# A mixture-of-experts pipeline: where silu and its product stand between the two halves of the next expert's gate and up weights

## The reference, cut to what matters

```python
xb = h[tok_b]
hid = jax.nn.silu(xb @ w_e_gate[e]) * (xb @ w_e_up[e])
return (hid @ w_e_down[e]) * w_b[:, None].astype(h.dtype)
```

## Time and profile before

| | |
|---|---|
| median of 3 runs | 3199.24 us (3198.63 to 3200.02) |
| the profiled execution | 3197.57 us, span 3195.9 us |
| PE busy | 2930.6 us, 92% of the span |
| DVE busy | 1774.6 us, 56% |
| ACT busy | 1414.9 us, 44% |
| POOL busy | 533.1 us, 17% |
| the experts' 64 blocks | about 1115 to 1752 us of the span |

### The profile page before, as it was taken

The page is one execution under the profiler, slowest core; times in us unless marked ns, Lnnn a source line. Parts: engine busy times, 40 slices in busy tenths (PEclk is TensorE's granted clock), DMA queues, the critical chain, the costliest instruction groups (busy, mean ns, idle before and its releaser), DMA issues. The chain is left out here.

```text
span 3195.9 us, 36485 instructions
## 1 busy us (share of the span) xinstructions
PE 2930.6 (92%) x14410; PEld 2346.5 (73%) x14410; DVE 1774.6 (56%) x2033; ACT 1414.9 (44%) x1832; POOL 533.1 (17%) x702
## 2 busy tenths in 40 slices
PE   7978899898998799999999679889999998889998
PEld 4856788787886387777777358678887797678887
DVE  4447745436544498888887253455544327455543
ACT  3324525336223188888787123433323225333322
POOL 0005514124101522222222100000000104000000
PEclk9989999998999799999999889999999999999999
DMA  5210101022652399999997632123332301223331
GB/s 199 60 55 1 56 32 54 27 54 73 211 191 92 114 338 365 364 370 370 373 373 304 261 113 93 53 81 92 105 105 66 96 27 54 73 80 93 93 105 40
DMA packets 276890, 455.94 MB, mean 143 GB/s; under 512 B 24400, under 2 KB 206288, under 8 KB 257648
## 3 DMA queue, kind: packets, MB, share of 16 engines
q1 hardware_dynamic: 250560, 398.82, 36.0%
q0 software_dynamic: 26160, 54.79, 4.8%
HBM read 450.63 MB, written 39.08 MB: 153 GB/s over the span
## 5 line engine op out<-in xcount | busy, mean ns | idle before, releaser
L253 DVE TENSOR_TENSOR weight_part<-weights,weight_part 128x2048 fp32r<-128x2048 f32 (+1 forms) x65 | 148.1, 2279 | 161.2 <-ACT weight_part L242 161.2
L1037 ACT ACTIVATE up_room<-banks,tap_columns 128x512 f32<-128x512 f32 x88 | 68.6, 779 | 314.0 <-PE banks L298 314.0
L293 PE MATMUL banks<-hT_r,weight_part 128*128 128x512 f32 x496 | 200.9, 405 | 4.6 <-PEq L878 2.9
L242 ACT ACTIVATE weight_part<-weights 128x2048 fp32r<-128x2048 f32 (+1 forms) x65 | 121.7, 1872 | 175.8 <-PE banks L293 169.9
L1078 DVE SCALAR_TENSOR_TENSOR up_room<-banks,tap_columns,up_room 128x511 f32<-128x511 f32 x88 | 65.9, 749 | 238.7 <-ACT up_room L1037 238.7
L298 PE MATMUL banks<-hT_r,weight_part 128*128 128x512 f32 x496 | 196.3, 396 | 0.0
L703 POOL TENSOR_SCALAR branch_mean<-branch_mean 128x1 f32<-128x1 f32 x20 | 4.4, 222 | 1113.2 <-ACT up_room L697 747.3
L293 PE MATMUL banks<-hT_r,weight_part_o 128*128 128x512 f32 x432 | 174.3, 403 | 7.1 <-PEq L110 4.2
L253 DVE TENSOR_TENSOR weight_part_o<-weights,weight_part_o 128x2048 fp32r<-128x2048 f32 (+2 forms) x49 | 106.9, 2181 | 129.5 <-ACT weight_part_o L242 129.5
L298 PE MATMUL banks<-hT_r,weight_part_o 128*128 128x512 f32 x432 | 170.5, 395 | 0.0
L297 PE MATMUL banks<-h_low,weight_part 128*128 128x512 f32 x432 | 169.7, 393 | 0.0
(11 more groups left out here) (704 smaller groups left out, 8746.3 us busy)
## 6 DMA issues: line engine op xcount, KB each, us to landing
weights<-in_w_e_gate SPq DMA_DIRECT2D x44, 1024.0 KB, 16.0
weights<-in_w_e_up SPq DMA_DIRECT2D x44, 1024.0 KB, 18.6
hT<-in_w_e_down SPq DMA_DIRECT2D x44, 1024.0 KB, 18.9
weights<-in_w_up SPq DMA_DIRECT2D x88, 512.0 KB, 5.1
gate_up<-in_w_e_gate SPq DMA_DIRECT2D x22, 1024.0 KB, 15.4
gate_up<-in_w_e_up SPq DMA_DIRECT2D x22, 1024.0 KB, 18.4
down<-in_w_e_down SPq DMA_DIRECT2D x22, 1024.0 KB, 18.8
weights<-in_w_down SPq DMA_DIRECT2D x20, 1024.0 KB, 5.0
```

Of the source, the lines that this page charges most:

```text
L242: c.nc.scalar.activation(self.parts[n % 2][0][:, 0:z], self.raw[n % RAW_SLOTS][:, 0:z], ACT.Copy).then_inc(self.high_ready, 1)
L253: c.nc.vector.tensor_tensor(low[:, 0:z], self.raw[n % RAW_SLOTS][:, 0:z], high[:, 0:z].bitcast(F32), ALU.subtract).then_inc(self.low_ready, 1)
L293: ins = c.nc.tensor.matmul(out, lhs[0], rhs[0], start=start, stop=False)
L1037: nc.scalar.activation(a[:, f % 2, v], c.ps[:, 2 * (f % 4) + v], ACT.Identity, scale=conv[:, 2, ch:ch + 1], bias=bias[:, ch:ch + 1]).then_ ...
```

## The change

In block n, ScalarE and VectorE now take the first half of block n + 1's gate and up weights ahead of silu and its product, and the second half behind them. What each instruction computes and the semaphores that it waits for and counts up are as before; TensorE, SyncE and GpSimd have the same lists.

```diff
-            def round_gate_up(n):
+            def round_half(n, v):
                 i = n % SETS
                 if n >= 2:
                     act.wait_ge(up_done, n - 1)
-                for v, landed in enumerate((gate_in, up_in)):
-                    act.wait_ge(landed[i], 16 * (n // SETS + 1))
-                    nc.scalar.activation(gu_high[n % 2][:, v], gu[i][:, v], ACT.Copy).then_inc(gu_rounded, 1)
+                act.wait_ge((gate_in, up_in)[v][i], 16 * (n // SETS + 1))
+                nc.scalar.activation(gu_high[n % 2][:, v], gu[i][:, v], ACT.Copy).then_inc(gu_rounded, 1)
...
                 if n + 1 < N:
-                    round_gate_up(n + 1)
+                    round_half(n + 1, 0)
                 if n < N:
                     act.wait_ge(up_done, n + 1)
                     if n >= 2:
                         act.wait_ge(gated, n - 1)
                     nc.scalar.activation(sl[n % 2][:], c.ps[:, n % 2, 0:EF], ACT.Silu).then_inc(silud, 1)
+                    if n + 1 < N:
+                        round_half(n + 1, 1)
                     round_down(n)
...
                 if n + 1 < N:
-                    part_gate_up(n + 1)
+                    part_half(n + 1, 0)
                 if n < N:
                     dve.wait_ge(silud, n + 1)
                     if n >= 2:
                         dve.wait_ge(hid_turned, n - 1)
                     nc.vector.tensor_tensor(hid[n % 2][:], sl[n % 2][:], c.ps[:, n % 2, EF:2 * EF], ALU.mult).then_inc(gated, 1)
+                    if n + 1 < N:
+                        part_half(n + 1, 1)
                     dve.wait_ge(d_rounded, n + 1)
```

More of the change, by code:

```diff
@@ L3331, in _ @@
                     nc.scalar.activation(by_row[:, tile, b * 64:(b + 1) * 64], c.ps[:, TURNED_AT[tile] + b].rearrange("p (q r) -> p q r", r=KD), ACT.Copy).then_inc(copied, 1)
-            round_gate_up(0)
+            for v in range(2):
+                round_half(0, v)
             for f in range(2):
@@ L3388, in _, with part_half @@
             hid_bank = c.ps[:, 2, 0:2 * P].rearrange("p (k n) -> p k n", n=P)
-            def part_gate_up(n):
+            def part_half(n, v):
                 i = n % SETS
-                for v in range(2):
-                    dve.wait_ge(gu_rounded, 2 * n + v + 1)
-                    nc.vector.tensor_tensor(gu_low[i][:, v], gu[i][:, v], gu_high[n % 2][:, v].bitcast(F32), ALU.subtract).then_inc(gu_parted, 1)
+                dve.wait_ge(gu_rounded, 2 * n + v + 1)
+                nc.vector.tensor_tensor(gu_low[i][:, v], gu[i][:, v], gu_high[n % 2][:, v].bitcast(F32), ALU.subtract).then_inc(gu_parted, 1)
             def part_x(n):
@@ L3502, in _ @@
             shared_gate(1)
-            part_gate_up(0)
+            for v in range(2):
+                part_half(0, v)
             for n in range(2):
```

## The result

The changed kernel takes **3236.24 us** (4 runs, 3233.06 to 3239.92) against 3199.63 us (3198.63 to 3202.61) of the kernel before: ratio 1.0115, 95% interval 1.0101 to 1.0129. The forecast was 3232, range 3222 to 3247. The profiled execution took 3238.21 us, span 3236.5 us.

The account below looks back on a forecast made before the run. TensorE was taken as the bound, with transfers at 0.96 in the middle stretch; the change adds a three-engine ring. +10.7, +16.1, +2.5 and +3.1 make +32.4 us, so 3199.24 becomes 3231.6, say 3232, range 3222 to 3247.

Parts of the forecast that it names:

- The ring: Each expert block: up product, then second half's rounding and low part behind silu, then next up product; 10.39 us per block.
- S + 4.59: Next up product's start, 4.59 us after S, when a block's up product is done; before, S + 3.61 in the early stretch.
- The three stretches: Added time: first 11 blocks (9.41 us each) +10.7, middle 49 (10.06) +16.1, last two (9.15) +2.5 us.
- The start: First block: next up product moves from 1122.89 to 1126.01, +3.1 us.
- The clock rival: Gaps in every block drop TensorE's clock, 1.6 us per fall: one block in four +25 us, all +99; chance 0.05.
- What stands behind the moved instructions: Later work on both engines still fits: ScalarE has 2.4 us to spare, VectorE's chain 0.2 us.
- Transfers at nothing: Weight transfers cost nothing, as slower blocks ask less of them; up weights land well under 19 us, DMA share about 0.92.
- The rival of late transfers on top: Late weights lengthen single blocks beyond 10.39 us: 16 blocks by 0.5 give +8, 3240 us; chance 0.12.
- the rival "hardly any change": Transfers alone set the middle stretch's 10.06 us and the ring is about 10.0: +11, 3210 us; chance 0.06.
- the wait at L3165: Middle stretch: hidden values' turning waits for the product of silu and up, 27 times, 23.3 us; removed but not gained.

Follow-up runs that it names:

- the first block as before: Changed kernel, but with the order of the kernel before in the first block (n = 0): 3232.34 us, ratio 1.0102.
- ScalarE's list alone: Kernel before with only ScalarE's list changed (second half behind silu), VectorE taking both halves and then the product: 3267.27 us, ratio 1.0218.
- the run without gathers: Changed kernel without the token gathers of blocks 4 to 63, computing on stale tokens: 3241.57 us, ratio 1.0135.
- VectorE's list alone: Kernel before with only VectorE's list changed (product between the halves), ScalarE rounding both halves before silu: 3199.76 us, ratio 1.0001.
- the runs with two pieces: Second half cut in two pieces: changed kernel with one TensorE wait 3200.12 us, with two waits 3196.32; order of the kernel before, two waits, 3199.37.
- the runs without gathers: Token gathers of blocks 4 to 63 left out: of the kernel before, 3172.85 us (ratio 0.9919), and of the changed kernel, 3241.57 us (1.0135).
- two pieces, one wait: Changed kernel with the second half in two pieces, TensorE waiting for all pieces at the up product's start: 3200.12 us, ratio 1.0003.

## Why the prediction was right, step by step

- **The ring.** Forecast S + 4.59 and 10.39 us per block; measured S + 4.62 and 10.45, and in the middle stretch no block lies outside 10.38 to 10.56. The links: 0.29, 1.91, 0.03, 2.29 and 0.10 for TensorE's start, which I had at 0.06 from the product's; the up product itself took 5.82 us instead of 5.80 (1203.63 to 1209.45).
- **The three stretches.** Forecast +10.7, +16.1 and +2.5 us. Blocks 1 to 11 took 1245.44 - 1127.95 = 117.49 us against 103.56, +13.9, of which 2.5 are the slow matmuls of block 1 (12.94 - 10.44); the middle stretch 512.18 - 492.99 = +19.2, the last two blocks 20.78 - 18.30 = +2.5. Without the slow matmuls the excess over the forecast, 0.7 and 3.1 us, is the 0.06 us per block.
- **The start.** Forecast +3.1 for the wait of the first block. It was mis-sized in one thing: the wait also dropped the clock, which the sum put at nothing. Up to block 1's up product the profiled execution lost 1127.95 - 1122.89 = 5.1 us. Of these 0.9 lay ahead of the blocks and 1.0 in block 0's up product, which ran at the lower clock for ten matmuls instead of four; both come before the moved half can act, and with the first block as before it was three matmuls. The other 3.2 are the wait, as forecast. Behind it come the 2.5 us of the slow matmuls. The clock rival priced a fall at 1.6 us with a chance of 5% and looked for it in the gaps of every block; it came in one place that I had not looked at. Everywhere else gaps of 0.8 us left the clock at 1.00: 61 of them in 637 us, and with ScalarE's list alone gaps of 1.3 us in every block did so too. The Trainium skill ("TensorE: Matmul & The Clock Gate", "A second HAM failure mode: psum-queue depth-cycling") reports for another kernel that short idles, when frequent enough, made the clock swing; it gives no length or rate for them, so this case doesn't contradict it, but no such swing occurred here.
- **How close the number is.** Forecast 3232, median 3236.24. The profiled execution is 2 us above that median: it took 3238.21 against a forecast of 3230.0 for it, 8.2 more, which the terms above add up to: 1.9 that is not the change's, 0.1 for the wait, 2.5 for the clock, 0.7 and 3.1 for the ring. The median lies only 4.6 us above its forecast of 3231.6, so a part of the closeness is chance between executions. The way, the ring and its size are not.
- **What stands behind the moved instructions.** VectorE waited 0.48 us for silu in the block shown, 0.2 was forecast; ScalarE had 2.46 us to spare, 2.4 forecast.
- **Transfers at nothing.** No wait of ScalarE for a transfer is left in 59 blocks, and the run without gathers moved neither stretch. The rival of late transfers on top didn't occur, and the DMA share is 0.93 where about 0.92 was forecast. Whether the up weights land well under 19 us, as forecast, the trace of the changed kernel can't say, for nothing waits for them. Of the rival "hardly any change" one half is true, that transfers set the 10.06 us; the other, a ring of 10.0, is not.
- **What the removal was worth.** The prediction called the wait at L3165 removed but not gained, because the up product needs the same half. VectorE's list alone and the runs with two pieces bear it out, for a deeper reason than mine: even with a shorter chain the middle stretch is the transfers'.

## What to carry to other kernels

A wait that the profile puts down to an instruction's place in a list is worth its removal only if what comes next on the waiting engine doesn't need the thing that was overtaken. Before moving work behind an instruction that waits, add up the path from what releases that wait back to it: here 4.6 us of ScalarE and VectorE were put into a loop that had 3.6 us of cover. And where transfers are queued near their limit, a wait for them is not evidence that a shorter chain would help: take some bytes away and see, as the runs without gathers did.

## What was not expected of the hardware

- A wait of 3.33 us on TensorE was followed by 12 matmuls at the lower clock (0.43 us apart instead of 0.23), while 61 waits of 0.8 us in 637 us left the granted clock at 1.00, and so did waits of 1.3 us in every block with ScalarE's list alone. Other gaps ahead of an up product: 2.31 us (before), 2.54 (two pieces, one wait), 3.32 (changed, no gathers) and 4.06 (ScalarE's list alone) were each followed by seven or so matmuls 0.43 us apart, one of 1.86 (VectorE's list alone) by none. After a gap of 1.94 us ahead of the last down product the clock had fallen in the run with one wait and not in the kernel before.
- Cutting a rounding of 128x2048 into two of 128x1024 cost 2.00 us instead of 1.92 on ScalarE, the low parts 2.36 instead of 2.29 on VectorE: 0.07 to 0.08 us for one more instruction.
